# A two-layer network on one core: fetched rows summed into residual rows, GpSimd out of the layer border, two weight splits moved ahead, fetches paced, and the head norm taken by columns

## The chip, the cores and the metric

The kernel runs on one core of a Trainium2 chip. The metric is the time of one execution on the device in microseconds (us), and the kernel before has three timed runs. Beside them there is one profiled execution, from which all rows below come.

The engines are called PE (matrix products), PEld (its weight loads), ACT (scalar engine), DVE (vector engine), POOL (GpSimd) and SP (which here only issues DMAs); "SPq" is SP's queue.

## What is computed

Everything is float32. 512 tokens of width 1024, with 16 learned meta tokens ahead of them, go through two layers.

```python
# layer 1
h = concat(meta, x)
h = h + mixer(rmsnorm(h, ln1_w)) @ w_out      # attention and a linear-attention branch
h = h[:, 16:]
hn = rmsnorm(h, ln2_w)
idx, gate = choose(hn)                        # 8 heads x 16 of 16384 experts per token
act = gelu(einsum('nd,nhkd->nhk', hn, u[idx]))
h = h + einsum('nhk,nhkd->nd', gate * act, v[idx])
x2 = rmsnorm(h, final_norm_w)
# layer 2
h = concat(meta_2, x2)
xn = rmsnorm(h, norm1_g)
...                                           # index attention, pooling and convolution branches
h = h + mixed @ w_o
h = h + swiglu(rmsnorm(h, norm2_g))
out = rmsnorm(h, final_g)
```

## The kernel before, in words

**Products.** A float32 product is made of three products of rounded halves: `split_products` (lines 208, 211 and 212) issues hi*hi, lo*hi and hi*lo. Each weight tile is loaded by SP as 128x1024 (512 KB), rounded to "hi" by ACT (`split_hi`: line 1501 in the experts, line 2123 in layer 2), and "lo" is the rest that DVE subtracts (`split_lo`, line 1638; `lower`, line 2431; in the first projection POOL does it, line 198). Four raw tiles (RAW) and three split ones (RING) are in flight. One such tile is one item of a stream; the order of the items is written out by hand in `expert_stream` and `second_stream`, and every engine runs through the same list and waits on counters.

**Head.** `phase_project_1` loads a gain column, the identity matrix and then x in four tiles of 128 rows and the meta rows (lines 539 to 543). DVE waits for all five before its first instruction of the norm. `RowStats` squares and sums each tile on ACT (358), takes the root there (363) and the reciprocal on DVE (376); `NormColumns` scales the rows (414), PE transposes them (445, meta rows 453) and ACT and DVE write hi and lo of each of the 8 column blocks (405, 424; meta 431 to 434). PE waits for all of it before the first projection `zT`.

**Experts.** The dense way is taken for 384 of the 512 tokens: each of 128 value tiles is an item of the `down` part (18 products, six banks). Ahead of each item DVE multiplies the loaded hidden values with gates (1743, 1745) and ACT and DVE split them (1543, 1749). The first 128 tokens go another way: POOL fetches, for pick r of each token, one hidden value (`fetch_own`, 1483) and one row of 1024 values (`fetch_row`, 1474) by indirect DMAs, and DVE adds the weighted row to `acc` (`mac`, 1768; the first one 1765). `macs_in` spreads the 128 of them over items 10 to 123 of `down`. POOL issues 16 hidden-value fetches at once, then rows and hidden values in turn; from the ninth row on a row fetch waits until an earlier row has been used (8 row slots).

**Border.** When the last products are made, DVE adds each of six banks to its half tile of 512 columns of the residual rows `h` (1808) and squares four of them (2443); POOL adds `acc` to tile 0 (2079), multiplies `h` by `final_norm_w` into `xg` (2082, 2086) and, after the statistics, writes x2 (2090); ACT squares `h` and `xg` (2197) and takes the root (2220). Then DVE and ACT scale two tiles each (2592, 2224), PE transposes (2380), ACT and DVE make hi and lo (2228, 2596), and item 0 of layer 2 begins. Its weights and those of item 1 are split after the last expert item. SP stores x2 (2061) when POOL is done.

**Second norm of layer 2.** Before item `silu 0` PE transposes the normed rows (`norm_2`, 445), and waits until all eight column blocks have hi and lo (405, 424).

## Time and profile before

| | us |
|---|---|
| timed runs, median of three | 2744.5 |
| lowest and highest of them | 2738.88, 2746.12 |
| profiled execution, own time | 2761.01 |
| its span in the trace | 2759.2 |
| PE busy in the span | 2634.4 (95%) |
| DVE / ACT / POOL busy | 1483.8 / 933.1 / 999.7 |

A start time in the rows is counted from the start of the span. A line number is one of the kernel before. "idle before" in brackets is how long the engine stood still ahead of the instruction, and what ended that.

### The profile page before, as it was taken

To read this page: it belongs to the slowest core of one execution; us is meant where nothing else is said; L and a number is where in the kernel's file an instruction comes from. 1 tells how busy PE (TensorE), PEld (TensorE's weight loads), DVE (VectorE), ACT (ScalarE), POOL (GpSimd) and SP (SyncE) were. 2 spreads that over 40 slices of the span, in tenths; PEclk is the share of its full clock that TensorE was granted. 3 is DMA by queue.
4 is the path that set the end of the run, shared out by engine and by line. 5 is a ranking of instruction groups with operands and counts; after the bars stand their busy time and mean duration, and the time that the engine had idled before them with its cause. 6 is when DMAs were issued, how large, how long until landed. Compare 5 with 4: busy or idle time off the path is not lost.

```text
span 2759.2 us, 33069 instructions
## 1 busy us (share of the span) xinstructions
PE 2634.4 (95%) x12445; PEld 2145.6 (78%) x12445; DVE 1483.8 (54%) x3027; ACT 933.1 (34%) x1436; POOL 999.7 (36%) x623
## 2 busy tenths in 40 slices
PE   7998889999999999998999999989998999899998
PEld 6776578888888888886888888867976677688886
DVE  4225736999563222224888888844973435333322
ACT  4222523333343222232333333433325532322212
POOL 3320020389886888305777775220240000000000
PEclk9997989999999999998999999999999999999999
DMA  4210136755667766557999999732321123233321
GB/s 131 83 31 4 42 120 210 244 122 142 135 175 189 148 143 146 147 186 236 358 358 362 356 359 364 255 97 76 85 84 46 39 76 130 69 97 94 99 93 68
DMA packets 330942, 427.83 MB, mean 155 GB/s; under 512 B 58720, under 2 KB 246912, under 8 KB 330272
## 3 DMA queue, kind: packets, MB, share of 16 engines
q1 hardware_dynamic: 271392, 358.39, 40.4%
q0 software_dynamic: 59392, 67.34, 10.6%
q8 instruction: 99, 1.62, 0.2%
q14 instruction: 59, 0.48, 0.1%
HBM read 362.59 MB, written 63.05 MB: 154 GB/s over the span
## 4 chain that ended last, share of the span: by engine, by line
PE 78%; DVE 3%; issue 2%; ACT 1%; POOL 0%; DMA 0%; SPq 0%; ACTq 0%; DVEq 0%
PE bank L208 25%; PE bank L211 25%; PE bank L212 25%; DVE s_wl L2431 1%; PE bank L1599 1%; PE bank L2371 1%; PE bank L1583 1%; ACT s_wh L2123 0%; PE bank L2329 0%; PE bank L2346 0%; PE bank L445 0%; PE bank L2369 0%; POOL s_xg L2086 0%; DVE s_score L2477 0%; DVE s_best L2473 0%
## 5 line engine op out<-in xcount | busy, mean ns | idle before, releaser
L1638 DVE TENSOR_TENSOR pe_wl<-pe_raw,pe_wh 128x1024 fp32r<-128x1024 f32 x272 | 353.9, 1303 | 475.2 <-ACT pe_wh L1501 446.1
L208 PE MATMUL bank<-pe_xh,pe_wh 128*128 128x512 f32 x1152 | 451.9, 392 | 1.1 <-DVE pe_xl L424 1.1
L212 PE MATMUL bank<-pe_xh,pe_wl 128*128 128x512 f32 x1152 | 448.6, 389 | 0.0
L211 PE MATMUL bank<-pe_xl,pe_wh 128*128 128x512 f32 x1152 | 448.3, 389 | 0.0
L1441 POOL DMA_INDIRECT scratch_sums<-pe_pick,pe_cell_u x256 | 414.8, 1620 | 89.8 <-issue 89.3
L1501 ACT ACTIVATE pe_wh<-pe_raw 128x1024 fp32r<-128x1024 f32 x272 | 287.6, 1057 | 342.3 <-PE bank L212 280.8
L2431 DVE TENSOR_TENSOR s_wl<-s_raw,s_wh 128x1024 fp32r<-128x1024 f32 x143 | 192.1, 1345 | 301.0 <-ACT s_wh L2123 299.7
L212 PE MATMUL bank<-pe_wh,pe_hl 128*128 128x512 f32 x768 | 304.2, 396 | 4.5 <-issue 4.5
L208 PE MATMUL bank<-pe_wh,pe_hh 128*128 128x512 f32 x768 | 304.6, 397 | 3.9 <-issue 3.8
L211 PE MATMUL bank<-pe_wl,pe_hh 128*128 128x512 f32 x768 | 304.2, 396 | 3.8 <-issue 3.8
L208 PEld LDWEIGHTS bank<-pe_xh,pe_wh 128*128 128x128 f32 x1152 | 216.4, 188 | 46.1 <-issue 1.0
L212 PEld LDWEIGHTS bank<-pe_xh,pe_wl 128*128 128x128 f32 x1152 | 216.2, 188 | 45.5
L211 PEld LDWEIGHTS bank<-pe_xl,pe_wh 128*128 128x128 f32 x1152 | 216.4, 188 | 44.0
L1513 ACT ACTIVATE pe_a_out<-bank 128x512 f32<-128x512 f32 x128 | 76.5, 598 | 482.6 <-PE bank L212 428.0
L1483 POOL DMA_INDIRECT pe_a_own<-scratch_hidden,pe_cell_u x128 | 174.2, 1361 | 146.6 <-DMA scratch_hidden<-pe_a_out 107.8
L2123 ACT ACTIVATE s_wh<-s_raw 128x1024 fp32r<-128x1024 f32 x143 | 149.9, 1049 | 164.1 <-PE bank L212 164.1
L1474 POOL DMA_INDIRECT pe_v_rows<-in_peer_v,pe_row_u x128 | 155.1, 1212 | 138.2 <-DVE pe_acc L1768 101.1
L208 PE MATMUL bank<-s_xh,s_wh 128*128 128x512 f32 (+2 forms) x536 | 194.7, 363 | 6.0 <-DVE s_wl L2431 4.4
L211 PE MATMUL bank<-s_xl,s_wh 128*128 128x512 f32 (+2 forms) x536 | 189.9, 354 | 0.0
L212 PE MATMUL bank<-s_xh,s_wl 128*128 128x512 f32 (+2 forms) x536 | 189.1, 353 | 0.0
L212 PEld LDWEIGHTS bank<-pe_wh,pe_hl 128*128 128x128 f32 x768 | 144.5, 188 | 41.3 <-issue 6.0
L211 PEld LDWEIGHTS bank<-pe_wl,pe_hh 128*128 128x128 f32 x768 | 144.6, 188 | 41.1 <-issue 5.7
(449 smaller groups left out, 4639.4 us busy)
## 6 DMA issues: line engine op xcount, KB each, us to landing
pe_raw<-in_peer_u SPq DMA_DIRECT2D x128, 512.0 KB
pe_raw<-in_peer_v SPq DMA_DIRECT2D x128, 512.0 KB
scratch_hidden<-pe_a_out SPq DMA_DIRECT2D x128, 256.0 KB
pe_a_in<-scratch_hidden SPq DMA_DIRECT2D x128, 192.0 KB
s_raw<-in_w_in SPq DMA_DIRECT2D x48, 512.0 KB, 3.9
s_raw<-in_w_gate_up SPq DMA_DIRECT2D x44, 512.0 KB, 3.9
scratch_sums<-pp_zeros SPq DMA_DIRECT2D x16, 1024.0 KB, 6.4
pe_added_gate<-scratch_sums SPq DMA_DIRECT2D x32, 512.0 KB
```

The costliest lines, as they stand in the source:

```text
L208: first = pe.matmul(out, lhs[0], rhs[0], start=start, stop=False, skip_group_check=skip)
L211: pe.matmul(out, lhs[0], rhs[1], start=False, stop=False, skip_group_check=skip)
L212: return pe.matmul(out, lhs[1], rhs[0], start=False, stop=stop, skip_group_check=skip)
L1441: pool.indirect_dma_start(cells, bass.IndirectOffsetOnAxis(ap=cell_u[:, t, at:at + 1], axis=0), pick[:, t, 2, at:at + 1], None, compute_op ...
L1474: pool.indirect_dma_start(v_rows[:, r % ROW_SLOTS, :], None, io["peer_v"].rearrange("n j d -> (n j) d"), bass.IndirectOffsetOnAxis(ap=row_ ...
L1483: pool.indirect_dma_start(a_own[:, r:r + 1], None, hidden.rearrange("n j (t one) -> (n j t) one", one=1), bass.IndirectOffsetOnAxis(ap=cel ...
L1501: act.activation(wh[:, i % RING, :], raw[:, i % RAW, :], ACT.Copy).then_inc(S["w_hi"], 1)
L1513: act.activation(a_out[:, n % 4, :], bank[:, A_BANK + i % 2, :], ACT.Gelu).then_inc(S["taken"], 1)
L1583: last = pe.matmul(bank[:, S_BANK + n % 2, t * P:(t + 1) * P], qT[:, n % 2, t * P:(t + 1) * P], keys[:, n, :], start=True, stop=True)
L1638: dve.tensor_tensor(wl[:, i % RING, :], raw[:, i % RAW, :], wh[:, i % RING, :].bitcast(F32), ALU.subtract).then_inc(S["w_lo"], 1)
L2123: act.activation(wh[:, i % RING, 0:width(i)], raw[:, i % RAW, 0:width(i)], ACT.Copy)\
L2431: dve.tensor_tensor(wl[:, i % RING, 0:width(i)], raw[:, i % RAW, 0:width(i)], wh[:, i % RING, 0:width(i)].bitcast(F32), ALU.subtract).then ...
```

## The change

1. Head: the meta rows and x are loaded ahead of gain and identity; DVE doesn't wait for all tiles; the meta rows are squared, scaled and transposed first (`meta_first`), into bank 7, whose token columns are transposed last; a Sqrt is issued on ACT ahead of the norm; the products of `zT` wait column block by column block.
2. Experts: rows are summed into `h[:, 0, :]`, `acc` is gone; OWN_PART is 8 instead of 16; the first 24 fetches wait for finished items.
3. Border: the splits of layer 2's items 0 and 1 are issued inside the last expert items (at `n == NB - 1`); SP loads four raw tiles of layer 2 there, not two; the products with `final_norm_w` are DVE's and the squares of `h` all ACT's; POOL writes x2 only after all column blocks are done; PE transposes the second half of the columns after the first column block's products of item 0.
4. `norm_2` writes into banks that begin with that of `silu 0`, which waits column block by column block.

```diff
 def on_tensor(self, pe, b, turn=0, between=None, ready=None):     # Gemm
+                if ready:
+                    ready(kt)
...
 class RowStats:
+        self.order = list(range(self.tiles))                      # [NT, 0, 1, 2, 3] with meta_first
...
         def _(sp):                                                # phase_project_1
+            sp.dma_start(h[0:META, NT, :], io["meta_tokens"]).then_inc(x_landed[NT], 16)
+            for t in range(NT):
+                sp.dma_start(h[:, t, :], io["x"][t * P:(t + 1) * P, :]).then_inc(x_landed[t], 16)
             sp.dma_start(gain[:, :], io["ln1_w"]).then_inc(g_landed, 16)
             sp.dma_start(const[:, 0:P], io["const"][:, 0:P]).then_inc(c_landed, 16)
...
+            act.wait_ge(S["zeroed"], 1)
+            act.activation(warm[96:P, :], w2[96:P, 0:1], ACT.Sqrt)
...
-            pe.wait_ge(norm.done, norm.total())
-            gemm.on_tensor(pe, zT_b)
+            gemm.on_tensor(pe, zT_b, ready=lambda kt: pe.wait_ge(norm.done, max(kt + 1, 2)))
...
-            for landed in x_landed:
-                dve.wait_ge(landed, 16)
...
-MACS_FROM, OWN_PART = 10, 16
+MACS_FROM, OWN_PART, PACED = 10, 8, 24
...
+            def pace():                                           # POOL, before each fetch
+                n = next(issued)
+                if n < PACED:
+                    pool.wait_ge(S["item_done"], DOWN + n * MACS_FROM // PACED)
...
+                if n == NB - 1:                                   # ACT, after split_hidden(n)
+                    ahead(act)
...
-                if r == 0:
-                    last = dve.tensor_scalar(acc[:, :], got, h_r, None, ALU.mult)
-                else:
+                if r:
                     dve.wait_ge(S["macs"], r)
-                    last = dve.scalar_tensor_tensor(acc[:, :], got, h_r, acc[:, :], ALU.mult, ALU.add)
-                last.then_inc(S["macs"], 1)
+                dve.scalar_tensor_tensor(h[:, 0, :], got, h_r, h[:, 0, :], ALU.mult, ALU.add).then_inc(S["macs"], 1)
...
+                if n == NB - 1:                                   # DVE, after split_hidden(n)
+                    ahead(dve)
...
-            ahead(dve)
+            own(dve)
...
-                if d >= 2:
-                    dve.wait_ge(S["rows_added"], d + 1)
-                    between(dve, d)
+                dve.wait_ge(S["rows_added"], d + 1)
+                weigh(dve, d)
...
-            for i in range(2):                                    # SP, layer 2
+            for i in range(RAW):
                 load(i)
             sp.wait_ge(life["gated"], PEER_KEYS)
...
-            for i in range(2, RAW):
-                load(i)
...
-            pool.wait_ge(life["macs"], PICKS)
-            pool.tensor_tensor(h_in[:, 0, :], h_in[:, 0, :], life["acc"][:, :], ALU.add).then_inc(S["own_added"], 1)
-            pool.wait_ge(S["gains_landed"], 16 * 3)
-            pool.wait_ge(S["own_added"], 1)
-            pool.tensor_tensor(xg[:, 0, :], h_in[:, 0, :], gain_row[:, :], ALU.mult).then_inc(S["gained"], 1)
-            for d in range(SIX):
-                t, half = 1 + d // 2, halves[d % 2]
-                pool.wait_ge(life["rows_added"], d + 1)
-                pool.tensor_tensor(xg[:, t, half], h_in[:, t, half], gain_row[:, half], ALU.mult).then_inc(S["gained"], 1)
-            pool.wait_ge(S["gained"], 1 + SIX)
-            pool.wait_ge(S["rstd"], 1)
+            pool.wait_ge(S["x_done"], KD)
             for t in range(NT):
                 pool.tensor_tensor(h_in[:, t, :], xg[:, t, :], rstd[:, 0, t:t + 1].to_broadcast([P, D]), ALU.mult)\
                     .then_inc(S["y_done"], 1)
...
                         if i == 0:                                # PE, products of a layer 2 item
+                            if kt == 1:
+                                turn_half(1)
                             pe.wait_ge(S["x_done"], kt + 1)
+                        if (kind, n) == ("silu", 0):
+                            pe.wait_ge(norm_2.done, kt + 1)
...
+        def scalar_ahead(act):
+            split_hi(act, 0)
+            split_hi(act, 1)
...
         def vector_ahead(dve):
+            lower(dve, 0)
+            lower(dve, 1)
+
+        def weigh_own(dve):
+            dve.wait_ge(S["gains_landed"], 16 * 3)
+            dve.wait_ge(life["macs"], PICKS)
+            dve.tensor_tensor(xg[:, 0, :], h_in[:, 0, :], gain_row[:, :], ALU.mult).then_inc(S["gained"], 1)
             dve.wait_ge(S["squared_m"], 1)
             dve.tensor_scalar(sum_m[:, :], sum_m[:, :], 1.0 / D, EPS, ALU.mult, ALU.add).then_inc(S["spread_m"], 1)
...
+        def weigh_rows(dve, d):
+            t, half = 1 + d // 2, halves[d % 2]
+            dve.tensor_tensor(xg[:, t, half], h_in[:, t, half], gain_row[:, half], ALU.mult).then_inc(S["gained"], 1)
```

## Rows read from the trace of the kernel before

**Rows 1.** Timeline of the head: start us, us, engine, line, instruction, count, idle before.
```profile
10.76 0.21 DVE L371 TENSOR_SCALAR pn_n_ss<-pn_n_ss 128x1 f32<-128x1 f32 x2 [9.27 <-DMA pn_h<-in_meta_tokens]
...
12.29 6.40 PE L445 MATMUL bank<-b1c_const,pn_h 128*128 128x128 f32 x32 [12.29 <-DVE pn_h L414]
...
17.95 4.73 ACT L405 ACTIVATE p_xh<-bank,p_gain 128x512 fp32r<-128x512 f32 x8 [1.94 <-PE bank L445]
18.74 5.36 DVE L424 SCALAR_TENSOR_TENSOR p_xl<-bank,p_gain,p_xh 128x512 fp32r<-128x512 f32 x8 [1.86 <-ACT p_xh L405]
...
24.94 0.59 PE L208 MATMUL bank<-p_xh,p_w_hi 128*128 128x264 f32 x1 [4.67 <-DVE p_xl L434]
...
32.11 0.80 DVE L791 COPY b1p_zT<-bank 128x264 f32<-128x264 f32 x2 [7.22 <-PE bank L212]
```
**Rows 2.** Products of the experts' down part: duration ns min/median/max, first and last start us.
```profile
L208 PE MATMUL bank<-pe_wh,pe_hh x768: 388/394/794, 1237.5 to 1793.3; 128*128 128x512 f32 x192
```
**Rows 3.** Timeline of the border, rows of all engines in order of time.
```profile
1767.56 1.06 SPq L2041 DMA_DIRECT2D s_raw<-in_w_index  x2
...
1777.48 2.51 DVE L1745 TENSOR_TENSOR pe_a_in<-pe_a_in,pe_gate 128x128 f32<-128x128 f32 x1
...
1781.64 1.06 ACT L1501 ACTIVATE pe_wh<-pe_raw 128x1024 fp32r<-128x1024 f32 x1 [1.09 <-PE bank L212]
...
1787.68 0.39 PE L208 MATMUL bank<-pe_wh,pe_hh 128*128 128x512 f32 x1
...
1792.24 0.68 DVE L1808 TENSOR_TENSOR b1r_h<-b1r_h,bank 128x512 f32<-128x512 f32 x1
...
1793.75 0.40 PE L212 MATMUL bank<-pe_wh,pe_hl 128*128 128x512 f32 x1
...
1799.76 0.63 ACT L2197 ACTIVATE s_junk<-s_xg 128x512 f32<-128x512 f32 x1 [0.50 <-POOL s_xg L2086]
...
1804.33 3.65 PE L2380 MATMUL bank<-b1c_const,s_xs 128*128 128x128 f32 x16 [10.18 <-ACT s_xs L2224]
...
1808.40 2.64 PE L2380 MATMUL bank<-b1c_const,s_xs 128*128 128x128 f32 x16 [0.42 <-DVE s_xs L2592]
...
1814.29 1.21 DVE L2431 TENSOR_TENSOR s_wl<-s_raw,s_wh 128x1024 fp32r<-128x1024 f32 x1
...
1816.64 0.60 ACT L2152 ACTIVATE s_qi<-bank 128x512 f32<-128x512 f32 x1 [3.64 <-PE bank L212]
```
**Rows 4.** Down part: us, busy of PE, PEld, DVE, ACT, POOL; clock, DMA share, GB/s.
```profile
1262.00:1292.00 30.00, 17.82 (x49) 11.48 (x49) 6.74 (x13) 5.47 (x8) 16.41 (x17) 0.66 0.64 198
...
1400.00:1450.00 50.00, 50.00 (x216) 40.09 (x215) 43.55 (x63) 17.50 (x25) 36.66 (x28) 1.00 0.97 350
```
**Rows 5.** POOL's fetches by line, 1241 to 1284 us: busy us, mean ns, idle before.
```profile
L1483 POOL DMA_INDIRECT pe_a_own<-scratch_hidden,pe_cell_u x24 | 25.1, 1046 | 114.8 <-DMA scratch_hidden<-pe_a_out 107.8 <-issue 7.0
L1474 POOL DMA_INDIRECT pe_v_rows<-in_peer_v,pe_row_u x8 | 7.5, 941 | 2.4 <-issue 2.4
```
**Rows 6.** Timelines of SP and ACT in the down part: a value tile's load, its split.
```profile
1249.38 0.43 SPq L1381 DMA_DIRECT2D pe_raw<-in_peer_v  x1
...
1286.40 1.06 ACT L1501 ACTIVATE pe_wh<-pe_raw 128x1024 fp32r<-128x1024 f32 x1 [19.75 <-DMA p_gain<-in_ln_w]
```
**Rows 7.** Timeline of `norm_2`.
```profile
2378.07 5.36 DVE L424 SCALAR_TENSOR_TENSOR s_fl<-bank,s_gain,s_fh 128x512 fp32r<-128x512 f32 x8 [2.56 <-ACT s_fh L405]
...
2383.48 0.80 PE L208 MATMUL bank<-s_fh,s_wh 128*128 128x512 f32 x1 [5.41 <-DVE s_fl L424]
...
2390.77 0.60 ACT L2139 ACTIVATE s_silu<-bank 128x512 f32<-128x512 f32 x1 [6.45 <-PE bank L212]
```
**Rows 8.** Issue to landing of the loads of x and of the meta rows.
```profile
DMA to landing us min/median/max: 3.9/5.6/7.1
```
**Rows 9.** Operations on `xg`: duration ns min/median/max, first and last start us.
```profile
L2592 DVE TENSOR_SCALAR s_xs<-s_xg,s_rstd x4: 486/2111/2117, 1801.7 to 1806.1; 128x512 f32<-128x512 f32 x4
L2090 POOL TENSOR_TENSOR b1r_h<-s_xg,s_rstd x4: 2069/2070/2127, 1801.8 to 1807.9; 128x1024 f32<-128x1024 f32 x4
```

More of the change, by code:

```diff
@@ L350, in on_scalar @@
     def on_scalar(self, act, ready):
-        for t in range(self.tiles + 1):
-            if t < self.tiles:
+        for j in range(self.tiles + 1):
+            if j < self.tiles:
+                t = self.order[j]
                 ready(act, t)
-                if t:
-                    act.wait_ge(self.squared, t)
+                if j:
+                    act.wait_ge(self.squared, j)
                 src, n = self.tile(t)
@@ L426, in on_vector @@
                 .then_inc(self.done, 1)
[L427 removed]
+        if self.meta is not None and not self.meta_first:
             dve.wait_ge(self.turned, KD + 1)
[L429 to L435 removed]
+            self.take_meta(dve, chain, 0).then_inc(self.done, 1)
@@ L437, in total, with take_meta @@
+    def take_meta(self, dve, chain, b):
+        src = self.bank[:, b, 0:KD * META].rearrange("p (k m) -> p k m", k=KD)
+        gain = self.gain[:, :].unsqueeze(2).to_broadcast([P, KD, META])
+        chain(dve.tensor_tensor(self.mtmp[:, :, :], src, gain, ALU.mult))
+        hi = self.hi[:, :, 0:META]
+        chain(dve.tensor_copy(hi, self.mtmp[:, :, :]))
+        return dve.tensor_tensor(self.lo[:, :, 0:META], self.mtmp[:, :, :], hi.bitcast(F32), ALU.subtract)
     def total(self):
-        return KD + (self.meta is not None)
+        return KD + (self.meta is not None and not self.meta_first)
@@ L440, in on_tensor, with turn_token @@
     def on_tensor(self, pe):
-        for t in range(NT):
-            pe.wait_ge(self.scaled, t + 1)
-            for k in range(KD):
-                last = pe.transpose(self.bank[:, (k + self.turn) % NBANK, t * P:(t + 1) * P], self.xs[:, t, k * P:(k + 1) * P],
-                                    self.ident)
-                if t == NT - 1:
-                    last.then_inc(self.turned, 1)
-        if self.meta is not None:
+        def turn_token(t, k):
+            last = pe.transpose(self.bank[:, (k + self.turn) % NBANK, t * P:(t + 1) * P],
+                                self.xs[:, t, k * P:(k + 1) * P], self.ident)
+            if t == NT - 1:
+                last.then_inc(self.turned, 1)
@@ new lines, in turn_meta @@
+        def turn_meta(b):
+            for k in range(KD):
+                last = pe.transpose(self.bank[:, b, k * META:(k + 1) * META],
+                                    self.xs[0:META, NT, k * P:(k + 1) * P], self.ident[0:META, 0:META])
+            return last
+        if self.meta_first:
+            pe.wait_ge(self.scaled, 1)
+            turn_meta(NBANK - 1).then_inc(self.meta_turned, 1)
+        for t in range(NT):
+            pe.wait_ge(self.scaled, t + 1 + self.meta_first)
+            for k in range(KD - self.meta_first):
+                turn_token(t, k)
@@ L450, in on_tensor @@
+        if self.meta_first:
+            pe.wait_ge(self.meta_done, 1)
+            for t in range(NT):
+                turn_token(t, KD - 1)
+        elif self.meta is not None:
             pe.wait_ge(self.scaled, NT + 1)
             pe.wait_ge(self.done, 1)
-            for k in range(KD):
-                last = pe.transpose(self.bank[:, 0, k * META:(k + 1) * META],
-                                    self.xs[0:META, NT, k * P:(k + 1) * P], self.ident[0:META, 0:META])
-            last.then_inc(self.turned, 1)
+            turn_meta(0).then_inc(self.turned, 1)
@@ L1629, in on_tensor, with on_vector @@
                 products(NB - 1, d).then_inc(S["rows_done"], 1)
-        def on_vector(dve, ahead, between):
+        def on_vector(dve, ahead, own, weigh):
             chain = Chain(dve, S["vector_steps"])
@@ L1974, in phase_second @@
         c_stats = RowStats(s, c, cm, "c_")
-        norm_2 = NormColumns(Scope(nc, ctx, "s2b"), h, None, gain_2, fh, fl, ident, bank, xs_2, junk_2)
+        norm_2 = NormColumns(Scope(nc, ctx, "s2b"), h, None, gain_2, fh, fl, ident, bank, xs_2, junk_2,
+                             turn=plan.banks[at["silu", 0]][0])
         last_stats = RowStats(s, h, None, "l_", junk=junk_2)
@@ L2394, in on_tensor @@
                     norm_2.on_tensor(pe)
-                    pe.wait_ge(norm_2.done, norm_2.total())
                 if i == at["index", 2]:
@@ L2700, in _ @@
             def _(act):
-                experts.scalar(act)
+                experts.scalar(act, layer.ahead[0])
                 layer.scalar(act)
@@ L2710, in _ @@
             def _(dve):
-                experts.vector(dve, layer.ahead, layer.between)
+                experts.vector(dve, *layer.ahead[1:])
                 layer.vector(dve)
```

132 lines of the change are left out of this document (62 added, 70 removed).

## The prediction

> **What bounds the kernel now.** I first read the page: PE is busy for 95% of the span, so only a stretch in which PE stands still or runs slowly can give time back. Then I asked for PE's waits over the whole span, longest first. The longest, 12.3 us, is at the head [rows 1], another of 10.2 us stands at the layer border [rows 3]. Neither is a wait for one slow instruction, so each was followed in the timeline. Last came a table of busy times by stretch, to find time lost between the waits.
>
> Head [rows 1]: DVE does nothing until the meta rows have landed, at 10.76. PE then turns 32 blocks until 18.69, ACT and DVE make the eight column blocks until 24.10, then come the meta rows, and the first product starts at 24.94. The result of `zT` is taken at 32.11.
>
> Experts: the products of the down part start at 1237.5 and the last ones at 1793.3 [rows 2]; the last product ends at 1794.15 [rows 3], so the part takes 556.6 us. Undisturbed it goes at 0.2335 us a product (26 steps from 1787.68 to 1793.75 [rows 3]), and 128 items of 18 products are 537.9 us. Thus 18.7 us are lost, all of them in one stretch: from 1262 to 1292 PE has 49 recorded products where 50 us of the steady state have 216 [rows 4]. That is when POOL has issued 24 hidden-value fetches and 8 row fetches within 42 us of 1241 [rows 5]. A value tile whose load was issued at 1249.38 was split at 1286.40, after ACT had stood still for 19.75 us [rows 6]: 37.0 us from issue to use. (The row names another DMA as releaser, but what ACT waits for there is this load.)
>
> Border [rows 3]: PE ends at 1794.15 and item 0 of layer 2 is taken at 1816.64. `norm_2` [rows 7]: PE waits 5.41 us for all eight column blocks.
>
> **Head, part by part.** The x tiles land 3.9 to 7.1 us after issue [rows 8], the last one issued at 3.1 at about 10.2. Issued some 0.45 us earlier it lands at 9.7; the identity matrix, now behind it, at about 10.4, and no transpose can start before. Until then ACT and DVE have done three tiles. 4 meta and token groups follow at 0.2 us a block (6.40/32 [rows 1]): meta 0.6, three tiles of seven blocks 4.2, so the first column block is turned at 10.4+0.6+4.2+0.2=15.4. From that to DVE's first lo it takes 0.8 (17.95 to 18.74 [rows 1]), and eight of them 5.36: done at 21.6. `zT` keeps up with them, but its last quarter waits for the weight slab that ACT can round only behind its eight hi's: 1.2 us more and 0.3 for the last products. `zT` ends at 22.9 instead of 32.1: **-9.2 us**. The ends: -6, if `zT` starts at the lower of PE's two clocks and isn't helped; -12, if the identity lands with the first x tile and the transposes aren't what is waited for. I take the value of the landing times, which are rows of the same loads. The Sqrt issued early costs nothing, ACT is idle then; the meta block's three DVE operations lie under the transposes. The four small loads that SP now issues a little later are wanted only after the second projection.
>
> **Experts.** Before, 32 fetches in 42 us; now 24 over ten items of 4.2 us, and only 8 rather than 16 hidden values ahead of the first row. That is one fetch in 1.75 us; the steady state [rows 4] has 28 POOL instructions in 50 us, or one in 1.8, and PE at full pace. The nearest row says that the stall goes: **-18.7 us** of the profiled execution; the other end is 0. What is queued behind the new wait on POOL are only later fetches. The eighth row is now issued at item 9 and first used at item 16, so DVE doesn't wait for it. Summing into `h` has the form of 127 of the 128 macs before; 8 more small weighings lie in DVE's 6.4 idle us of 50 [rows 4].
>
> How much of the 18.7 the timed runs have is not shown. The profiled execution takes 2761.01, 16.5 above the median 2744.5, and no other stretch of the trace is lost time of that size; so the timed runs may hold between 2.2 (all the gap is this stall) and 18.7. I take about half, **-10 us** against the median.
>
> By the Trainium skill (DMA: Bandwidth & Descriptors, "Queues, rings and completion order") each DMA engine serves its queue rows in turn, a packet at a time, so a second queue would take turns with SP's loads and not shut them out. By it POOL's fetches alone would not hold a load for 37 us, and the pacing would give nothing.
>
> **Border.** The early splits: ACT and DVE have their free time between 1778.9 and 1781.6, when ACT next waits for PE [rows 3]; two splits of 1.0 on ACT fit, and DVE's two of 1.2 end near 1782.5, just ahead of its last expert split. DVE also loses its 2.5 us instruction at 1777.48 [rows 3], which ran while POOL added `acc`. Per bank DVE then has an add of 0.68 [rows 3] and a product of the same size, 1.4 in all, as much as PE needs for a bank (6 products of 0.2335). So the last bank is added at 1794.9 and weighted at 1795.6, its last square starts at 1795.7 against 1799.76: 4.1 earlier. From there to the scaling takes 1.94 [rows 3, 9] and stays. The scaling before was 2.65 to the first transpose, as three of DVE's four took 2.11 beside POOL's 2.07 [rows 9]; alone they take 0.49, and ACT's two of 0.65 set 1.3: another 1.3 earlier. The first transpose is at 1799.0 instead of 1804.33, -5.3. Both halves are still 3.65+2.64, with one block's products (0.7 to 1.3) between them and the lo's of the last four blocks, 0.67 each, behind: about +0.6. Item 0 ends 4.7 earlier.
>
> Against that stands what moved: POOL's four products of 2.07 came at 1801.8 and now come behind the last column block, at 1808.2 to 1816.5, where DVE must scale the meta rows and split items 2 and 3 (1.21 each [rows 3]). By [rows 9] a DVE operation beside such a one takes 2.1 instead of 0.5. Item 2 would begin at 1817.3; five short DVE operations, each behind one of POOL's, end between 1814 and 1820.5. I take 1.2 us of delay, so **-3.5 us** for the border, ends -5.5 and -1.5. SP waits for POOL ahead of its x2 store, with the load of item 7 behind it; that is wanted some 20 us later.
>
> The Trainium skill's rule (SBUF — State Buffer, "Who interferes with whom") is that DVE in a two-port mode or with two SBUF inputs and GpSimd exclude each other for a whole instruction. The 2.11 beside 2.07 agrees. It speaks for the removed part and against the moved one.
>
> **norm_2.** PE may start when the first lo is done, 2378.07+0.67=2378.74 instead of 2383.48, and DVE's 0.67 a block is about PE's 0.70 (three products of 0.2335). The item ends at 2378.8+5.6+0.3=2384.7 against 2390.6 [rows 7]: **-5.9 us**, of which 4.7 are the start and the rest the slow products (0.43 and more apart) that followed the wait. Ends -4.5 and -6.3. The next item's weights are already split, and the one after it is split at 2384.6, in time.
>
> **Sum.** Profiled execution: 2761.0-9.2-18.7-3.5-5.9=2723.7. Timed: 2744.5-9.2-10-3.5-5.9=2715.9, called 2716.
>
> **Rivals.**
> *The pacing gives the timed runs nothing* (the stall wasn't there, or stays by the rule above): 2744.5-18.6=2725.9. For it: the 16.5 us gap. Against: the fetches and the stall coincide. Chance 0.27.
> *The stall is whole in the timed runs and goes*: 2744.5-9.2-18.7-3.5-5.9=2707.2. For it: the timed runs do the same DMAs. Against: then the gap has no place. Chance 0.18.
> *Port for port at the border*: POOL's late products stop DVE as long as possible, up to 1820.5, and head and border give only their lower ends: 2715.9+3.2+2.0=2721. Chance 0.09.
> *Slower: the early split waits for its load.* The splits of layer 2's first items stand in ACT's queue ahead of the last expert split, wanted at 1781.64; their load is issued at 1767.56 [rows 3]. If it lands as late as the one of [rows 6], 37.0 after issue, at 1804.6, the last two expert items stand 23.0 us. With the pacing worth nothing this gives 2744.5-18.6+23.0=2749; it turns slower from a landing 32.7 us after issue (14.1 of slack and 18.6). For it: two more loads are issued together. Against: no row fetch is open by then. Chance 0.02.
>
> My forecast has 0.44. The likeliest case's own range is 2708 to 2724. The range 2701 to 2729 takes in the two near rivals with a few us of the head's and border's bounds. A measurement of this kernel tells about 0.3% (8 us) from no change: faster 0.95, same 0.03, slower 0.02.
>
> **What would show it.** Right: first product near 17 and `zT` taken at 23; no wait of ACT for a load at 1250 to 1290 and a down part of 538 to 540 us; 17.5 us from the last expert product to item 0's end instead of 22.4; `silu 0` starting 0.8 us behind the transposes. Wrong: a down part that still has a stretch at the low clock; DVE's splits of items 2 and 3 taking over 2 us; a first product that waits for ACT's hi.

## The result, and the profile after

The changed kernel takes 2723.47 us (median of four runs, 2721.22 to 2725.97) against 2744.66 for the kernel before (four runs, 2738.88 to 2746.12): a ratio of 0.993, with a 95% interval of 0.9916 to 0.9944. The medians are 21.2 us apart. The profiled executions are 39.8 us apart (2761.01 and 2721.22). Most of what follows is about these 18.6 us that the profiles show and the timed runs don't. Most of them are a stall of the kernel before that appears in the runs on one chip and not in those on another.

The page of the changed kernel, its span and its first part:

```profile
span 2719.4 us, 33076 instructions
## 1 busy us (share of the span) xinstructions
PE 2623.9 (96%) x12445; PEld 2140.9 (79%) x12445; DVE 1484.9 (55%) x3034; ACT 935.9 (34%) x1444; POOL 995.0 (37%) x615
```

PE is busy for 10.5 us less than before, the other engines about as long. What has gone is time in which PE stood still or was slow. The products of the down part, as [rows 2], and two of the stretches of [rows 4] (us, busy of PE, PEld, DVE, ACT and POOL, clock, DMA share, GB/s):

```profile
L208 PE MATMUL bank<-pe_wh,pe_hh x768: 393/396/398, 1225.5 to 1762.4; 128*128 128x512 f32 x192
```

```profile
1262.00:1292.00 30.00, 30.00 (x131) 24.15 (x130) 23.55 (x37) 10.54 (x14) 18.64 (x15) 1.00 0.96 343
1400.00:1450.00 50.00, 50.00 (x216) 40.29 (x215) 43.50 (x65) 17.91 (x24) 36.80 (x27) 1.00 0.98 355
```

From the first product to the last one's start it is 536.9 us where it was 555.8, and 1262 to 1292 looks like any other stretch. The head, as [rows 1], from the timeline:

```profile
9.42 1.03 PE L468 MATMUL bank<-b1c_const,pn_h 16*128 16x16 f32 x8 [9.42 <-DMA b1c_const<-in_const]
10.38 5.67 PE L460 MATMUL bank<-b1c_const,pn_h 128*128 128x128 f32 x32
...
17.29 0.36 PE L208 MATMUL bank<-p_xh,p_w_hi 128*128 128x264 f32 x1 [1.24 <-issue]
...
23.00 0.80 DVE L821 COPY b1p_zT<-bank 128x264 f32<-128x264 f32 x2 [1.86 <-PE bank L212]
```

The first product is 7.65 us earlier and `zT` 9.11; PE's first instruction now waits for the identity matrix. The other 1.46 us are the pace of `zT`'s own 48 products: before, the first ones were 0.22 us apart behind PE's 4.67 us of standing still, at the lower clock (the granted clock is 0.78 from 25 to 32); now PE has stood still for 1.24 us only, the clock is 1.00, and they are 0.12 apart from the first on. The border, as [rows 3, 9], from the timeline of all engines:

```profile
1766.63 1.67 DVE L2630 TENSOR_SCALAR s_xs<-s_xg,s_rstd 128x512 f32<-128x512 f32 x4
...
1768.01 3.67 PE L2413 MATMUL bank<-b1c_const,s_xs 128*128 128x128 f32 x16 [4.78 <-ACT s_xs L2252]
...
1772.57 1.91 PE L2413 MATMUL bank<-b1c_const,s_xs 128*128 128x128 f32 x16
...
1776.80 10.11 POOL L2118 TENSOR_TENSOR b1r_h<-s_xg,s_rstd 128x1024 f32<-128x1024 f32 x4 [60.01 <-DVE s_xl L2634]
...
1779.40 0.60 ACT L2184 ACTIVATE s_qi<-bank 128x512 f32<-128x512 f32 x1 [2.83 <-PE bank L212]
...
1780.98 2.33 DVE L2465 TENSOR_TENSOR s_wl<-s_raw,s_wh 128x1024 fp32r<-128x1024 f32 x1 [2.37 <-ACT s_wh L2150]
...
1785.18 1.88 DVE L2649 TENSOR_TENSOR s_xl<-s_mtmp,s_xh 128x128 fp32r<-128x128 f32 x1
```

DVE's four scalings take 1.67 us where three of them took 2.11 each. PE's last expert product ends at 1763.24, so item 0 is taken 16.2 us later where it was 22.5. These 6.3 us can be followed along the chain. From the start of the last L208 product of the experts (1793.29 before, 1762.37 now) to the first scaling it is 4.3 us where it was 8.4; from there to the first transpose 1.4 where it was 2.7; the rest, 0.9, lies between the transposes and item 0. The first and largest part, 4.1, ends before any scaling starts. It is the product with `final_norm_w`, on which the last squares wait: POOL took 1.71 us for a half tile (median), DVE takes 0.69. POOL's four products stand where the prediction put them, behind the column blocks, and DVE's operations beside them are long: 2.33 for a split of 1.21, item 3's (item 2's, at 1777.41, still took 1.21). `norm_2`, as [rows 7]:

```profile
2344.39 5.36 DVE L437 SCALAR_TENSOR_TENSOR s_fl<-bank,s_gain,s_fh 128x512 fp32r<-128x512 f32 x8 [2.11 <-ACT s_fh L415]
...
2345.28 0.47 PE L208 MATMUL bank<-s_fh,s_wh 128*128 128x512 f32 x1 [0.89 <-DVE s_fl L437]
...
2351.06 0.60 ACT L2171 ACTIVATE s_silu<-bank 128x512 f32<-128x512 f32 x1 [0.41 <-PE bank L212]
```

PE waits 0.89 us for one lo in the place of 5.41 for eight. Between the two profiled executions the gain is 9.1 us at `zT`, 12.1 at the experts' first product (408.5 and 396.4), 30.9 at their last, 35.6 at layer 2's index scores, 33.2 at the end of `wo` and 39.8 at the end.

### The profile page after: what moved, and what is told of

It reads as the page before. It is cut to its first block, busy times and chain, and to the rows that moved or that the text cites. A ratio compares the mean times of both kernels' runs of the same rounds, so it can differ in the third digit from the quotient of the medians.

```text
span 2719.4 us, 33076 instructions
## 1 busy us (share of the span) xinstructions
PE 2623.9 (96%) x12445; PEld 2140.9 (79%) x12445; DVE 1484.9 (55%) x3034; ACT 935.9 (34%) x1444; POOL 995.0 (37%) x615
## 3 DMA queue, kind: packets, MB, share of 16 engines
q0 software_dynamic: 59392, 67.34, 10.5%
## 4 chain that ended last, share of the span: by engine, by line
PE 80%; DVE 3%; ACT 2%; issue 1%; ACTq 0%; DVEq 0%
PE bank L208 25%; PE bank L211 25%; PE bank L212 25%; DVE s_wl L2465 1%; PE bank L1640 1%; PE bank L2403 1%; PE bank L1624 1%; ACT s_wh L2150 0%; PE bank L2361 0%; PE bank L2378 0%; PE bank L2401 0%; PE bank L460 0%; DVE s_score L2516 0%; DVE s_best L2512 0%; ACT L2166 0%
## 5 line engine op out<-in xcount | busy, mean ns | idle before, releaser
L208 PE MATMUL bank<-pe_xh,pe_wh 128*128 128x512 f32 x1152 | 451.9, 392 | 1.4 <-DVE pe_xl L437 1.3
L208 PE MATMUL bank<-pe_wh,pe_hh 128*128 128x512 f32 x768 | 303.7, 396 | 0.0
L208 PEld LDWEIGHTS bank<-pe_xh,pe_wh 128*128 128x128 f32 x1152 | 216.4, 188 | 46.3 <-issue 1.2
L1512 POOL DMA_INDIRECT pe_a_own<-scratch_hidden,pe_cell_u x128 | 180.3, 1409 | 147.7 <-DMA scratch_hidden<-pe_a_out 107.9
L208 PE MATMUL bank<-s_xh,s_wh 128*128 128x512 f32 (+2 forms) x536 | 196.0, 366 | 7.4 <-DVE s_wl L2465 4.4
```

The costliest lines, as they stand in the source:

```text
L208: first = pe.matmul(out, lhs[0], rhs[0], start=start, stop=False, skip_group_check=skip)
L1512: pool.indirect_dma_start(a_own[:, r:r + 1], None, hidden.rearrange("n j (t one) -> (n j t) one", one=1), bass.IndirectOffsetOnAxis(ap=cel ...
```

## The experiments

Twelve programs ran, four at a time, on three chips, which the results name as 8, 9 and 12. Unchanged runs of the kernel before were taken beside each four; "before" is their median. The changed kernel itself ran beside none of them: its 2723.47 us are those of the first comparison, and where a variant is set against them, the two were not measured side by side.

**1 to 4, on chip 8 (before: 2741.94, 22 runs, 2736.94 to 2746.66).** The question was the prediction's least certain term, the pacing.

Experiment 1, the changed kernel without it:

```diff
-MACS_FROM, OWN_PART, PACED = 10, 8, 24
+MACS_FROM, OWN_PART, PACED = 10, 8, 0
```

> The changed kernel with the pacing alone taken out (PACED 0; 8 hidden values still go first). Theory A: the 18.9 us stall of the profiled execution of before is not part of its timed runs, so the pacing is worth at most 2 us there: 2723 to 2726, whatever the profile shows. Theory B: the timed runs have it and the pacing removed it, and something else gave about 16 us back: 2735 to 2743. In the profile, if the stall comes from the burst of fetches, the down part takes 545 to 557 us against 537.8 with pacing; if 8 instead of 16 early values was what mattered, 538.

Measured: 2723.6 us (2720.66 to 2725.39), ratio 0.9937 (0.9923 to 0.995), as the first theory has it. Its down part lasts 536.9 us from first to last start, without a stall.

Experiment 2, the kernel before with the pacing and with 8 hidden values fetched ahead, and nothing else:

```diff
-MACS_FROM, OWN_PART = 10, 16
+MACS_FROM, OWN_PART, PACED = 10, 8, 24
...
+                pace()
                 fetch_own(r)
...
+                pace()
                 fetch_row(r)
```

> The kernel before with the pacing and the parts of 8 alone. Theory A: 2742 to 2745, no difference from before. Theory B: 2725 to 2730. The profile should have a down part of 538 us by both if the burst makes the stall.

Measured: 2744.11 us (2737.98 to 2747.41), ratio 1.0006 (0.9997 to 1.0015): no gain that can be measured.

Experiment 3, the kernel before, unchanged, profiled a second time (no edit):

> The kernel before, unchanged, profiled once more. If the stall belongs to the kernel and its burst, its profile again has a down part of 550 to 557 us and a time near 2761; if it was an accident of one execution, 538 us and 2742. The timed runs should be 2739 to 2746 and tell the spread of a kernel against itself.

Measured: 2742.52 us (ratio 1.0004, 0.9994 to 1.0013). Its trace, products of the down part and the stretch of [rows 4]:

```profile
L208 PE MATMUL bank<-pe_wh,pe_hh x768: 393/396/398, 1240.1 to 1777.0; 128*128 128x512 f32 x192
```

```profile
1262.00:1292.00 30.00, 30.00 (x130) 24.18 (x129) 19.00 (x33) 11.02 (x16) 23.57 (x22) 1.00 0.95 335
```

POOL issues the same burst (busy 23.57 of 30), and PE doesn't lose a tenth of a microsecond.

Experiment 4, the kernel before with a larger burst, 32 hidden values ahead:

```diff
-MACS_FROM, OWN_PART = 10, 16
+MACS_FROM, OWN_PART = 10, 32
```

> The kernel before with 32 instead of 16 hidden values fetched at once, some 20 us more of fetches at one in 1.25 us. Theory A: timed 2740 to 2747, as before, since the timed runs don't stall on the burst. Theory B: a stall that grows with the burst, 2755 to 2765 timed, and a down part over 570 us in the profile.

Measured: 2749.67 us (2745.83 to 2751.25), ratio 1.0034 (1.0021 to 1.0047), 7.7 us more than before, between the ranges of the two theories; in the trace the down part is 542.0 us, 5.1 more. The waits from 1284 to 1300 show where they go:

```profile
DVE pe_h_own L1756 <- DMA pe_a_own<-scratch_hidden,pe_cell_u: 4.9, 1, 4.9
PEld bank L208 <- DVE pe_wl L1638: 3.7, 1, 3.7
```

DVE stands still until the fetched hidden values of the first part have landed, now 32 of them, and then waits for the rows; the lo of the next value tile stands behind that in DVE's order, and PE waits for it. So on this chip too a burst can cost time, by making DVE wait for what it fetches, and 16 ahead is still below that. After these four I took the 18.7 us for an accident of one execution. That was premature.

**5 to 8, on chip 9 (before: 2754.11, 7 runs, 2750.6 to 2757.93).** Four variants of the changed kernel at the border and at `norm_2`. The surprise was in the comparison: unchanged runs of the kernel before took 12.2 us more than on chip 8, while variants of the changed kernel stayed at 2720 to 2724.

Experiment 5, POOL's products a step later:

```diff
-            pool.wait_ge(S["x_done"], KD)
+            pool.wait_ge(S["x_done"], KD + 1)
```

> The changed kernel with one wait of GpSimd later: its product of the fetched rows with the row scale (the y product, 10.11 us in four instructions, from 1776.80) starts one step of the normalised rows later, after the last of them, the memory rows' (L2634). Theory A, my prediction's: item 2's lateness (it is taken 7.46 us after item 1, 5.80 in the kernel before) is the price of the y product lying beside VectorE's splits and casts (2.33, 1.60 and 1.88 us, against 0.2 to 1.2 without it). Then moving it by the time of one VectorE step moves the collision rather than removing it: the time stays within 2 us of the changed kernel's 2723.5. Rival B: the collision only costs because it holds the last two casts of the normalised rows (L2648, L2649), which TensorE waits 1.4 us for: if these go first, 1.4 to 1.7 us come back, 2722.

(The step waited for is the memory rows' lo, L2649; the expectation names L2634, the column blocks', which is what the changed kernel waits for.) Measured: 2722.08 us (2717.98 to 2723.48), ratio 0.988 (0.9863 to 0.9896). Timeline:

```profile
1783.86 0.60 ACT L2184 ACTIVATE s_qi<-bank 128x512 f32<-128x512 f32 x1 [2.80 <-PE bank L212]
...
1785.44 1.23 DVE L2465 TENSOR_TENSOR s_wl<-s_raw,s_wh 128x1024 fp32r<-128x1024 f32 x1 [2.34 <-ACT s_wh L2150]
...
1787.16 0.29 DVE L2649 TENSOR_TENSOR s_xl<-s_mtmp,s_xh 128x128 fp32r<-128x128 f32 x1
...
1787.60 7.45 POOL L2118 TENSOR_TENSOR b1r_h<-s_xg,s_rstd 128x1024 f32<-128x1024 f32 x4 [66.38 <-DVE s_xl L2649]
```

The split is back at 1.23, the lo at 0.29 instead of 1.88, POOL's four take 7.45 instead of 10.11, PE's wait of 1.4 us for L2649 is gone, and item 2 is taken 5.80 us after item 1 instead of 7.46. The trace bears out the second theory: the collision moved to where nobody waits. The time of 2722.08 us lies in the ranges of both.

Experiment 6, the same products as early as their data allow, beside DVE's scalings, where the kernel before had them:

```diff
-            pool.wait_ge(S["x_done"], KD)
+            pool.wait_ge(S["rstd"], 1)
```

> The changed kernel with the same y product of GpSimd started as soon as the row scale is there, so beside VectorE's four scalings of the fetched rows (0.23 us for a half tile where they run alone; 6.58 us for all in the kernel before, 1.67 in the changed one, where GpSimd is out of their way). Theory A (GpSimd beside VectorE is what the border's gain came from): the scalings go back to some 5 us, item 0 comes 3 to 5 us later and item 2 1.7 sooner: slower by 1.5 to 3.5 us, 2725 to 2727. Rival B (the gain at the border came from the work GpSimd no longer does, the sum of the fetched rows ahead of the squares, and not from who runs beside whom): within 1 us of 2723.5.

Measured: 2720.32 us (2718.12 to 2732.12), ratio 0.9874 (0.9857 to 0.989). By its times the misplaced products cost nothing, and 2720.32 lies below the ranges of both theories. Its trace, of the execution that took 2732.12 us, shows what they do:

```profile
1775.93 6.59 DVE L2630 TENSOR_SCALAR s_xs<-s_xg,s_rstd 128x512 f32<-128x512 f32 x4
1776.04 8.22 POOL L2118 TENSOR_TENSOR b1r_h<-s_xg,s_rstd 128x1024 f32<-128x1024 f32 x4 [49.94 <-DVE s_rstd L2625]
```

1.67 us have become 6.59, to the hundredth what the kernel before had in experiment 3 (6.58, beside 8.22 of POOL). Item 0 is taken 20.9 us after the start of the last L208 product of the experts where it was 17.0 in the changed kernel: 3.9 later. Item 2 gets 1.66 back. The net 2.2 us are less than the runs differ among themselves (14 us here), so the collision is shown by the trace alone, and the timed comparison neither supports it nor denies it. Nor does the trace decide all for the first theory. The first scaling starts 4.3 us after that product, as in the changed kernel, where it was 8.4 in the kernel before (7.5 in experiment 3's trace): with POOL back beside the scalings, the largest part of the border's gain is still there. That part is work that GpSimd no longer does, as the rival has it, though the products with `final_norm_w` and not the sum of the fetched rows set it. And the 3.9 us are more than the collision cost before, since the changed kernel puts a column block's products between the two halves of the transposes.

Experiment 7, `silu 0` waiting for all eight column blocks again:

```diff
-                            pe.wait_ge(norm_2.done, kt + 1)
+                            pe.wait_ge(norm_2.done, KD)
```

> The changed kernel with the first product after the second norm waiting for all eight columns blocks of the normalised rows again, as in the kernel before; nothing else altered. Theory A: the norm's gain in the trace, 6.5 us (-33.2 at the end of the product ahead of it, -39.8 at the end of the kernel), is TensorE's start on the first blocks while VectorE still transposes the later ones: slower by 5 to 6.5 us, 2729 to 2730. Rival B: part of that gain is only another window of low clock after it, so that the whole wait costs under 4 us.

Measured: 2729.42 us (2726.85 to 2731.15), ratio 0.991 (0.9893 to 0.9926), 6.0 above the changed kernel, with no overlap of the runs, and 6.3 to 9.1 above the medians of the other three on chip 9. PE's timeline:

```profile
2349.84 0.77 PE L208 MATMUL bank<-s_fh,s_wh 128*128 128x512 f32 x1 [5.50 <-DVE s_fl L437]
2350.41 0.63 PE L211 MATMUL bank<-s_fl,s_wh 128*128 128x512 f32 x1
2350.84 0.63 PE L212 MATMUL bank<-s_fh,s_wl 128*128 128x512 f32 x1
```

The start is 4.5 us later, and the products behind the wait are 0.43 apart instead of 0.23. The first theory holds.

Experiment 8, the splits of items 0 and 1 behind the last expert item again:

```diff
-                if n == NB - 1:                     # ACT and DVE, in the last expert items
-                    ahead(act)
...
+            scalar_ahead(act)                       # ACT, ahead of layer 2's norm; DVE likewise
```

> The changed kernel with the weight splits of items 0 and 1 put back behind the last expert item, where the kernel before has them; the split is then in the stretch between TensorE's last expert product and its first product of item 0. Theory A: the early splits are a part of the border's gain (6.3 us at item 0, of which the prediction gave some 2 to 3 to the splits that no longer stand ahead of the norm's pieces on ScalarE and VectorE): slower by 2 to 4 us, 2725.5 to 2727.5. Rival B: the chain through the norm sets item 0 and the splits fit beside it anyway: within 0.7 us of 2723.5, and the border's gain is GpSimd's work alone.

Measured: 2723.12 us (2721.08 to 2725.54), ratio 0.9886 (0.987 to 0.9903). In the trace item 0 is 17.4 us behind the last expert product's start, 17.0 in the changed kernel: the rival holds, the early splits are worth 0.4 us. (The expectation has the prediction give 2 to 3 us to them; it had given them none.) The border's gain is POOL's absence, from the products with `final_norm_w` first and from DVE's scalings second.

**9 to 12, on chip 12 (before: 2759.19, 13 runs, 2754.24 to 2765.53).** The pacing once more, which the 12 us of chip 9 had called for.

Experiment 9, the kernel before a third time (no edit):

> The kernel before, unchanged, profiled again, because its unchanged runs beside the last four experiments took 2754.1 us where beside the first four they took 2741.9, while the changed kernel's variants took 2720 to 2724 in both. Theory A: the stall of the down part (row 4, 18.7 us in the first profile, none in the second) comes more often on some chips than on others; where unchanged runs take about 2754, this trace shows the down part lasting 545 to 557 us rather than 537.8. Rival B: the 12 us lie in another part, such as the attention part's stretches of low clock, and the down part lasts 537.8 again. Where the unchanged runs take about 2742, both expect 537.8 and nothing is told apart.

Measured: 2757.64 us (2752.8 to 2762.11, 10 runs), ratio 0.999 (0.998 to 1.0001). Its trace:

```profile
L208 PE MATMUL bank<-pe_wh,pe_hh x768: 392/394/785, 1241.1 to 1795.5; 128*128 128x512 f32 x192
```

```profile
1262.00:1292.00 30.00, 19.40 (x61) 11.98 (x60) 4.46 (x8) 4.02 (x6) 19.80 (x20) 0.76 0.75 238
```

The stall is there in the same 30 us as in [rows 4]: 61 products where experiment 3 has 130, and a DMA rate of 238 GB/s where it has 335. From first to last start the down part takes 554.4 us, 17.5 more than the 536.9 of chip 8, and the timed runs are 17.3 above that chip's. ACT's timeline shows its splits late:

```profile
1266.59 1.06 ACT L1501 ACTIVATE pe_wh<-pe_raw 128x1024 fp32r<-128x1024 f32 x1 [6.98 <-PE bank L212]
...
1279.46 1.06 ACT L1501 ACTIVATE pe_wh<-pe_raw 128x1024 fp32r<-128x1024 f32 x1 [11.40 <-DMA p_gain<-in_ln_w]
...
1290.92 1.06 ACT L1501 ACTIVATE pe_wh<-pe_raw 128x1024 fp32r<-128x1024 f32 x1 [9.99 <-DMA p_gain<-in_ln_w]
```

Value tiles are split 8.5, 12.9 and 11.5 us apart where an item takes 4.2. But they are not what PE stands still for. What it waited for from 1240 to 1300 (weight loads, us in all, times, longest):

```profile
PEld bank L212 <- issue: 6.1, 4, 2.6
PEld bank L211 <- issue: 5.8, 7, 1.9
PEld bank L208 <- issue: 4.1, 5, 1.7
```

"issue" is time in which the engine waited for nothing that the profile shows, and in experiment 3 the same view is empty. The program has PE wait only ahead of an item's 18 products. Counted off 18 to an item, the eighth item had its last input, its lo, at 1268.90, but its products start from 1271.48 to 1287.26, over 15.8 us where 3.97 are usual; the ninth had its lo at 1281.78, began at 1288.66 and took 7.5. In the first trace of the kernel before it is the same: the eighth item had its lo at 1267.50 and its products start over 17.2 us. Three rows of PE's timeline out of the middle of them:

```profile
1280.72 0.58 PE L212 MATMUL bank<-pe_wh,pe_hl 128*128 128x512 f32 x1 [1.52 <-issue]
1282.13 0.58 PE L208 MATMUL bank<-pe_wh,pe_hh 128*128 128x512 f32 x1 [0.83 <-issue]
1284.23 0.59 PE L211 MATMUL bank<-pe_wl,pe_hh 128*128 128x512 f32 x1 [1.52 <-issue]
```

Nor were bytes of the loads held back in that trace. From 1249 to 1268 SP's queue starts 509 packets of 4096 bytes, a load has 128, and the four loads issued from 1245.21 to 1257.78 are through with them, the one of [rows 6] among them. From 1273 to 1290 only POOL's queue moves anything (packets, MB, share of 16 engines):

```profile
q0 software_dynamic: 974, 2.81, 53.6%
```

Its last packets start at 1285.4, and at 1286.40 ACT goes on. So PE loses its time product by product, while the rows that POOL fetched are moving. ACT's late splits run beside that: had PE kept its pace, it would have stood for the ninth item's lo instead, which came at 1288.72 in the first trace and at 1281.78 in this one. What holds PE, and what holds ACT's split of a tile whose bytes are there, no run here shows.

Experiment 10, the kernel before with pacing and 8 ahead (the edit of experiment 2):

> The kernel before with the pacing of the fetches and 8 rows ahead alone, as in the second experiment. Theory A (the stall, and its end by pacing): where unchanged runs take about 2754, this one takes about 2742 to 2744, a gain of 10 to 12 us that was not there beside the first four experiments. Rival B (the 12 us are elsewhere): it takes as long as the unchanged kernel, within 3 us. Where unchanged runs take about 2742: 2744 by both.

Measured: 2738.63 us (2736.78 to 2742.17), ratio 0.9927 (0.9904 to 0.9949): 20.6 us less than before, by the edit that gave nothing on chip 8, and more than the 10 to 12 that the first theory had.

```profile
L208 PE MATMUL bank<-pe_wh,pe_hh x768: 393/396/398, 1237.8 to 1774.7; 128*128 128x512 f32 x192
```

```profile
1262.00:1292.00 30.00, 30.00 (x130) 24.17 (x129) 19.45 (x33) 10.43 (x14) 18.86 (x16) 1.00 1.01 362
```

536.9 us again. Experiment 11, the changed kernel without pacing (the edit of experiment 1):

> The changed kernel without the pacing of its first 24 fetches. Theory A: where unchanged runs of the kernel before take about 2754, this one has the burst and so the stall: 2730 to 2736, where the changed kernel's variants took 2722 to 2723.5. Rival B (8 rows ahead in the place of 16, or something else of the change, is enough): 2721 to 2725, as in the first experiment. Where unchanged runs take about 2742: 2723.5 by both.

Measured: 2728.82 us (2727.65 to 2739.0), ratio 0.9902 (0.9874 to 0.993).

```profile
L208 PE MATMUL bank<-pe_wh,pe_hh x768: 393/394/793, 1225.6 to 1771.9; 128*128 128x512 f32 x192
```

546.3 us: 9.4 of the stall remain, again inside PE's items (18 products over 8.7 and 8.1 us). 2728.82 lies between the ranges of theory and rival. So there seem to be two parts to the cure: the waits remove these 9.4 us, and something that the changed kernel has without them removes the other half. That it is the 8 ahead rather than 16 is likely, but not shown, as this kernel differs from the one before in more than that. This run also shows that experiment 1 was right and yet not general.

Experiment 12, two improvements on the changed kernel: the edit of experiment 5, and the identity loaded ahead of x.

```diff
             sp.dma_start(h[0:META, NT, :], io["meta_tokens"]).then_inc(x_landed[NT], 16)
+            sp.dma_start(const[:, 0:P], io["const"][:, 0:P]).then_inc(c_landed, 16)
             for t in range(NT):
...
-            sp.dma_start(const[:, 0:P], io["const"][:, 0:P]).then_inc(c_landed, 16)
```

> The changed kernel with two edits: GpSimd's y product one step later, as in the fifth experiment (item 2 taken 5.80 us after item 1, 7.46 without it), and the load of the transposes' identity issued ahead of the x loads. In the changed kernel's trace TensorE's first instruction waits 9.4 us for that load. Theory A: the identity is the head's first limit, and with it landed by about 5 us the first transposes come with the scaled rows, some 0.5 to 1.5 us earlier, which the table of zT follows: 1.7 + 1 = 2 to 3 us less than 2723.5, about 2721. Rival B: the first x lands later by the identity's transfer, and the scaled rows are late in its place: no gain at the head, 1 to 2 us in all, about 2722.

Measured: 2718.54 us (2716.43 to 2721.41), ratio 0.9851 (0.9829 to 0.9873), the lowest of the study. PE's head:

```profile
7.97 1.00 PE L468 MATMUL bank<-b1c_const,pn_h 16*128 16x16 f32 x8 [7.97 <-DVE pn_h L424]
9.17 6.14 PE L460 MATMUL bank<-b1c_const,pn_h 128*128 128x128 f32 x32 [0.20 <-DVE pn_h L424]
...
16.46 0.36 PE L208 MATMUL bank<-p_xh,p_w_hi 128*128 128x264 f32 x1 [1.14 <-issue]
```

The transposes begin 1.21 us earlier and now wait for scaled rows; `zT` is taken at 22.18, 0.82 earlier, and item 2 comes 5.80 us after item 1. Both halves of the first theory are in the trace. The changed kernel itself didn't run on chip 12, so the 4.9 us between 2718.54 and 2723.47 are not a comparison on one chip; what the trace supports is 0.8 at the head and 1.7 at the border.

## Why the prediction was right, and where it was not

Forecast 2716.0, measured 2723.5: inside the range of 2701 to 2729, and the sign was right. But the cause of the 7.5 us between them is one of its terms, the pacing, and the likeliest case was not the one that came. That the forecast lies so near is in part luck, since its largest term was a guess of one half and rested on a wrong account of the stall.

One execution's positions shift with the attention part's stretches of low clock: the experts' first product stands at 408.4 to 412.0 in the six traces of the kernel before and its variants, and at 396.3 to 405.7 in seven of the changed kernel and its variants (experiment 12 left out). The terms below therefore compare means of stretches, not two traces.

**Head, predicted -9.2 (-6 to -12).** Measured -9.1 at `zT`, first product at 17.3 where it said "near 17". The landing times of the x loads were the right rows; the identity landed at 9.4, 1.0 earlier than I had it. One term did not come: the last quarter of `zT` was to wait 1.2 us for its weight slab. PE's `zT` products start without a pause from 17.29 on, 0.12 apart, and it is their number, 5.7 us of them, that sets the end at 23.0. Without that term the sum would have ended at 21.7; that it comes within a tenth of a microsecond is chance. No experiment undoes the head, but in experiment 12, where the first product is 0.83 earlier, `zT` is 0.82 earlier. At the experts the mean gain is 10.7 us (409.9 and 399.2). The 12.1 of the two profiled executions holds 1.4 of chance.

**Pacing, predicted -18.7 of the profiled execution and -10 of the timed runs.** The first is right in size, 18.9 by the starts, and a down part of 536.9 us is the same in every trace without a stall. Its mechanism is not. The prediction read a load that came 37.0 us after its issue, and so PE short of a tile. The split was that late, but the trace shows the tile's bytes moved by 1268, and there and in experiment 9 PE stands still inside items that had all their inputs. That the burst is what brings the stall on holds: experiment 10 takes it away on chip 12. The step that failed in size is "I take about half, -10 us against the median". The 18.7 us were not spread over executions in part: chip 8 has none of it, in 32 runs and one trace, and chip 12 has 17.5, in 23 runs and one trace. Of the first comparison's 21.2 us, head (10.7), border (3.2) and `norm_2` (6.1) make 20.0, all by means of traces. That leaves 1.2 us for the stall, under the lower end of the 2.2 to 18.7 that the prediction had; against chip 8's 18.3 us without any stall (experiment 1) it leaves 2.9. The rival "the pacing gives the timed runs nothing", 2725.9, is what those timed runs and chip 8 show; the rival "the stall is whole in the timed runs and goes" is what chip 12 shows. Its "against", that the gap of 16.5 us between profile and median would have no place, missed that the profiled execution and the timed runs need not have been made under the same conditions. That they were on two chips is likely, as three chips gave three medians of the same kernel, but the results for the first runs don't say so. Nor is it shown that the chip itself is what differs: each was used in one session only, and where the program's data lay in memory, or what else changed between sessions, was not varied.

The rule of the Trainium skill that was weighed there (DMA: Bandwidth & Descriptors, "Queues, rings and completion order"), by which a second queue takes turns with SP's loads and doesn't shut them out, agrees with chip 8: from 1270 to 1285 of experiment 3's trace SP's queue moves 2.65 MB and POOL's 2.26. The stalled traces don't contradict it, as the loads' bytes were not held back there. What the prediction drew from it, that the pacing would then give nothing, fails on chip 12, where it gives 20.6 us: the stall was of another kind than the one that the rule speaks of.

**Border, predicted -3.5 (-5.5 to -1.5).** From the last expert product's start to `wo`'s first product it is 528.2 us in the mean of six traces of the kernel before and its variants, and 525.05 in four with the changed border (525.9, 525.0, 526.0, 523.3): -3.2. The two halves were right in kind, each a little small: item 0 gained 6.3 between the two traces (predicted 4.7; 5.1 against experiment 3, whose own item 0 was 1.2 earlier than that of [rows 3]), and POOL's late products cost 1.66 (predicted 1.2). The parts of the first half came where they were put: 4.1 ahead of the last square (predicted 4.1), 1.3 between scaling and first transpose (1.3), and 0.9 gained behind it where 0.6 was to be lost. The early splits were costed at nothing, as work that fits where it is, and that held (0.4 gained, experiment 8). DVE beside POOL in the scalings is the smaller part, but a live one: experiment 6 puts item 0 back by 3.9 us with one wait. One of the prediction's own signs of being wrong, a split of items 2 and 3 over 2 us, did come, for item 3 (2.33), and by itself it proved nothing. The Trainium skill's rule on DVE and GpSimd (SBUF — State Buffer, "Who interferes with whom") agrees: 6.59 us for four operations that take 1.67 alone. "Port for port at the border" overstated the moved products; DVE was stopped, but ahead of PE's need it lost only 1.66.

**`norm_2`, predicted -5.9 (-4.5 to -6.3).** From `wo`'s end to item `silu 0` taken it is 17.7 us (2333.37 to 2351.06) where it was 24.2, so -6.5 between the two traces; undone, it costs 6.0 in timed runs, and by means of the traces it is 6.1. The predicted mechanism, 4.7 of start and the rest from slow products behind the wait, is what the rows of experiment 7 show.

**The slow rival**, the early split that waits for its load, didn't come: ACT splits items 0 and 1 at 1747.91, in 2.00 us, and its next expert split follows at 1750.73.

**Left open.** Between the index scores and the end of `wo` 2.4 us of the pair's gain are lost. Some 1 us is PE's step in `wo`: its L208 products have a median of 397 ns in this trace and 388 in [rows 3]'s, but over the other traces both kernels show 388, 394 and 397, so it isn't the change's. What makes PE stand still between products in the stall, with its inputs there, is open, and so is why chips (or sessions) differ under the burst: no experiment here looked at either. On chip 9 no trace of the kernel before was taken, so its 12.2 us are put down to the stall by analogy only.

## What to carry to other kernels

A stall in one profile that the median doesn't have may come and go with the chip or the session: run the unchanged kernel on more than one before a cure is called useless, or worth its full size. A burst of small gathers beside a saturated load stream is worth pacing even where it seems harmless; the pacing cost nothing measurable on chip 8 and gave 20.6 us on chip 12. When a late operand stands beside an idle engine, check that the engine lacked it: here an item's inputs were there, and PE idled inside the item. Where GpSimd and VectorE share a stretch, place GpSimd's instructions by who waits for VectorE there: one wait, moved by one step, took 1.7 us off the border, and moved to the other side it put 2.2 on.

## What the runs showed of the hardware that was not expected

- The same program has medians of 2741.9, 2754.1 and 2759.2 us in its runs on three chips. With the pacing it has 2744.1 on chip 8 and 2738.6 on chip 12, and the changed kernel's paced variants, `norm_2` undone left out, lie within 2720.3 to 2723.1 on chip 9 and at 2718.5 on chip 12.
- Under 32 indirect fetches in about 42 us PE stands still for up to 2.3 us at a time between products that wait for nothing the profile shows, in the traces of 17.5 and 18.7 us of stall, and not at all in the one of chip 8. PE's granted clock in the stretch is 0.66 and 0.76 there and 1.00 on chip 8.
- With half the head start of the fetches (8 in place of 16, in the changed kernel) 9.4 us of stall remain where the kernel before has 17.5. The 5.1 us that 32 ahead cost on chip 8 are another thing: DVE waits 4.9 us for the fetched values.
